# Forgetting-attention logits as three products of reduced-precision halves, with the halves made by ScalarE and GpSimd a pair of heads at a time

## The chip, the cores and the metric

The kernel runs on one NeuronCore of a Trainium2 chip. The metric is the device time of one execution in microseconds (us); smaller is better. Five engines run their own instruction queues in order and meet only at semaphores: TensorE (PE in the profile, its weight loads PEld), VectorE (DVE), ScalarE (ACT), GpSimd (POOL) and SyncE (SP, which here issues nearly all the DMAs).

## The reference

One block of a streaming encoder, batch 1, 512 tokens, 1024 channels, float32. A shared input projection feeds two branches, an mLSTM with 4 heads of 128 and a forgetting attention with 8 heads of 64; gates merge them, and an output projection and a SwiGLU feed-forward follow. The change touches only the logits of the second branch:

```python
def forgetting_attention(q, k, v, log_f):
    scale = q.shape[-1] ** -0.5
    cum = jnp.cumsum(log_f, axis=-1)
    for blk in range(s // Q_BLOCK):          # Q_BLOCK = 128
        lo = blk * Q_BLOCK; hi = lo + Q_BLOCK
        logits = (jnp.einsum("bhtd,bhsd->bhts", q[:, :, lo:hi], k[:, :, :hi]) * scale
                  + (cum[:, :, lo:hi, None] - cum[:, :, None, :hi]))
        mask = (lo + jnp.arange(Q_BLOCK))[:, None] >= jnp.arange(hi)[None, :]
        p = jax.nn.softmax(jnp.where(mask, logits, -jnp.inf), axis=-1)
        outs.append(jnp.einsum("bhts,bhsd->bhtd", p, v[:, :, :hi]))
```

## The kernel before

Weights stream from memory as granules of 128 x 1024 values into two staging buffers. ACT copies each granule to a tile of the reduced type fp32r (`w_hi`, L506), DVE subtracts that from the whole value and gets the rest, also fp32r (`w_lo`, L778), into a ring of four. PE then multiplies in three products, high by high, high by low and low by high (`three`, L1218 to L1220), each one instruction. The scores of the mLSTM heads are made in the same way from `q_hi`, `q_lo`, `k_hi`, `k_lo`.

The attention logits are not. `q_f` and `k_f` hold the scaled queries and the keys of all four pairs of heads as plain float32, a pair of heads on the 128 partitions, 64 each. `fox_logits(v)` (v = 0 to 15; pair of heads hp = v // 4, query block q) multiplies n = 128(q + 1) keys for both heads: one float32 product per head (L1442), recorded as two instructions each, on the upper and the lower 64 rows of the array; then one fp32r product per head that adds the forget-gate rows (`rows_both`, L1446), then the causal mask (L1449). The query blocks follow one another as q = 0, 1, 2, 3, 3, 2, 1, 0, so that n is 128, 256, 384, 512, 512, 384, 256, 128, twice over. Two of the eight PSUM banks are used by each step, four in turn.

On PE the order is written by hand. After the last mLSTM head (`mlstm_values(3)`, L1416) come `fox_logits(0)`, four k-steps of an output-gate projection, `fox_logits(1)`, and then `gate_piece`s: 32 pieces of three products each, of the first four gate granules, which fill the loop below. A granule's first piece takes bank 7 and waits until ACT has read the former granule out of it (`first_gate_tanh`, L644).

```python
for v in range(FOX_PAIRS):            # 16 steps
    fox_transpose(v)                  # L1463, waits for DVE's division of the probabilities
    if v + 2 < FOX_PAIRS: fox_logits(v + 2)
    if v == 0: mlstm_transpose(3)     # L1425
    for _ in range(FILL[v]): gate_piece(next(pieces))
    fox_values(v)                     # L1480, signals fox_pv
```

DVE's turn of step v: `fox_take_high` (L1059), for v = 0 `take_ymT(3)` (L944, L946, the output of the last mLSTM head), `fox_divide(v + 1)` (L1047, L1049), `fox_row_max(v + 2)` (L1036), for v = 1, 2, 6, 10 a weight half (L778). ACT's turn: for v = 2, 6, 10 the gate tanh (L644), `fox_take_low` (L640), for v = 0 `take_ymT_hi(3)` (L591), for v = 1, 2, 6, 10 a weight half (L506), `fox_softmax(v + 2)` (L630, two exponentials with their sums). POOL is nearly idle: in the mLSTM stage it squares each head's output (L472, 128 x 512) and takes a power of four values per partition (L465). ACT reaches the stage after `k_f` (L582), the floor of the stabiliser (L587) and the decays of the mLSTM heads (L609, L591, L506, L597).

## Time and profile before

| | |
|---|---|
| median of 3 runs | 780.4 us (778.96 to 780.73) |
| the profiled execution | 781.96 us |
| its span on the core | 780.2 us, 9668 instructions |
| PE busy | 768.6 us (99%) |
| DVE, ACT, POOL busy | 373.2, 257.6, 24.9 us |
| granted TensorE clock, mean | 0.996 of full |

The busy time of PE is a sum of pipelined records whose ends are modelled; what a stretch costs is read from the starts of its records or from the chain of waits. The attention stage lies between 193 and 258 us from the start of the span.

### The profile page before, as it was taken

To read this page: it belongs to the slowest core of one execution; us is meant where nothing else is said; L and a number is where in the kernel's file an instruction comes from. 1 tells how busy PE (TensorE), PEld (TensorE's weight loads), DVE (VectorE), ACT (ScalarE), POOL (GpSimd) and SP (SyncE) were. 2 spreads that over 40 slices of the span, in tenths; PEclk is the share of its full clock that TensorE was granted. 3 is DMA by queue.
4 is the path that set the end of the run, shared out by engine and by line. 5 is a ranking of instruction groups with operands and counts; after the bars stand their busy time and mean duration, and the time that the engine had idled before them with its cause. 6 is when DMAs were issued, how large, how long until landed. Compare 5 with 4: busy or idle time off the path is not lost.

```text
span 780.2 us, 9668 instructions
## 1 busy us (share of the span) xinstructions
PE 768.6 (99%) x3925; PEld 632.6 (81%) x3925; DVE 373.2 (48%) x561; ACT 257.6 (33%) x422; POOL 24.9 (3%) x50
## 2 busy tenths in 40 slices
PE   8999999999999999999999999999999999999996
PEld 7888888888576788888889888888888888888885
DVE  4678625357878525244355444433434445123224
ACT  5444222344555332233243323222323323213121
POOL 5000000012100000000000000000000000000000
PEclk9999999999999999999999999999999999999999
DMA  7324324210111134332311423332333323322302
GB/s 216 122 98 138 125 91 132 86 49 29 55 56 56 52 99 176 105 108 93 123 55 55 138 79 107 108 90 74 107 109 108 108 67 118 125 71 87 127 1 108
DMA packets 61776, 75.11 MB, mean 96 GB/s; under 512 B 3666, under 2 KB 49826, under 8 KB 61732
## 3 DMA queue, kind: packets, MB, share of 16 engines
q1 hardware_dynamic: 61728, 74.50, 29.8%
q8 instruction: 31, 0.51, 0.3%
q14 instruction: 13, 0.11, 0.0%
q10 hardware_dynamic: 4, 0.00, 0.0%
HBM read 72.40 MB, written 2.10 MB: 95 GB/s over the span
## 4 chain that ended last, share of the span: by engine, by line
PE 72%; issue 1%; DVE 0%; ACT 0%; POOLq 0%; POOL 0%; DVEq 0%; ACTq 0%
PE bank L1218 23%; PE bank L1219 22%; PE bank L1220 22%; PE bank L1480 1%; PE bank L1442 1%; PE bank L1463 1%; PE bank L1449 0%; PE bank L1231 0%; PE bank L1446 0%; ACT square_out L487 0%; DVE probs L1049 0%; ACT x L740 0%; DVE x L1190 0%; ACT ymT_hi L591 0%; DVE work L944 0%
## 5 line engine op out<-in xcount | busy, mean ns | idle before, releaser
L1218 PE MATMUL bank<-hT_hi,w_hi 128*128 128x512 f32 (+1 forms) x680 | 259.5, 382 | 1.6 <-DVE w_lo L778 1.1
L778 DVE TENSOR_TENSOR w_lo<-stage,w_hi 128x1024 fp32r<-128x1024 f32 x125 | 152.4, 1224 | 225.3 <-ACT w_hi L506 216.8
L1219 PE MATMUL bank<-hT_lo,w_hi 128*128 128x512 f32 (+1 forms) x680 | 256.7, 378 | 0.0
L1220 PE MATMUL bank<-hT_hi,w_lo 128*128 128x512 f32 (+1 forms) x680 | 256.5, 377 | 0.0
L506 ACT ACTIVATE w_hi<-stage 128x1024 fp32r<-128x1024 f32 x127 | 133.4, 1053 | 124.4 <-PE bank L1220 120.1
L1218 PEld LDWEIGHTS bank<-hT_hi,w_hi 128*128 128x128 f32 x680 | 128.2, 189 | 25.4 <-DVE w_lo L778 1.5
L1220 PEld LDWEIGHTS bank<-hT_hi,w_lo 128*128 128x128 f32 x680 | 128.1, 188 | 23.4
L1219 PEld LDWEIGHTS bank<-hT_lo,w_hi 128*128 128x128 f32 x680 | 128.3, 189 | 22.5
L1218 PE MATMUL bank<-w_hi,aT_hi 128*128 128x512 f32 x176 | 68.5, 389 | 0.0
L1220 PE MATMUL bank<-w_hi,aT_lo 128*128 128x512 f32 x176 | 68.5, 389 | 0.0
L1219 PE MATMUL bank<-w_lo,aT_hi 128*128 128x512 f32 x176 | 68.5, 389 | 0.0
L725 ACT ACTIVATE aT_hi<-work 128x512 fp32r<-128x512 f32 x22 | 13.9, 633 | 99.3 <-DVE work L1171 99.3
L1220 PEld LDWEIGHTS bank<-w_hi,aT_lo 128*128 128x128 f32 x176 | 33.1, 188 | 6.9
L1218 PEld LDWEIGHTS bank<-w_hi,aT_hi 128*128 128x128 f32 x176 | 33.1, 188 | 6.9
L1219 PEld LDWEIGHTS bank<-w_lo,aT_hi 128*128 128x128 f32 x176 | 33.1, 188 | 6.7
L721 ACT ACTIVATE work<-bank 128x512 f32<-128x512 f32 x22 | 13.2, 598 | 68.7 <-PE bank L1220 68.7
L1167 DVE SCALAR_TENSOR_TENSOR work<-work,bank 128x512 f32<-128x512 f32 x22 | 15.1, 688 | 38.5 <-PE bank L1220 38.4
L1218 PE MATMUL bank<-w_hi,mixT_hi 128*128 128x512 f32 x64 | 25.2, 393 | 0.0
L1218 PE MATMUL bank<-w_hi,hT_hi 128*128 128x512 f32 x64 | 25.2, 393 | 0.0
L445 POOL TENSOR_TENSOR rstd<-mean_sq,minus_half 128x1 f32<-128x1 f32 x12 | 6.6, 552 | 573.7 <-DVE mean_sq L749 573.3
L1220 PE MATMUL bank<-w_hi,hT_lo 128*128 128x512 f32 x64 | 24.9, 390 | 0.0
L1220 PE MATMUL bank<-w_hi,mixT_lo 128*128 128x512 f32 x64 | 24.9, 390 | 0.0
(190 smaller groups left out, 759.6 us busy)
## 6 DMA issues: line engine op xcount, KB each, us to landing
stage<-in_w_in SPq DMA_DIRECT2D x21, 1024.0 KB, 5.2
stage<-in_w_gate SPq DMA_DIRECT2D x11, 1024.0 KB, 5.3
stage<-in_w_up SPq DMA_DIRECT2D x11, 1024.0 KB, 5.4
stage<-in_w_down SPq DMA_DIRECT2D x22, 512.0 KB, 4.5
stage<-in_w_out SPq DMA_DIRECT2D x4, 1024.0 KB, 5.0
x_nat<-in_x SPq DMA_DIRECT2D x4, 512.0 KB, 5.7
stage<-in_w_br_mlstm SPq DMA_DIRECT2D x4, 512.0 KB, 3.5
stage<-in_w_br_fox SPq DMA_DIRECT2D x4, 512.0 KB, 4.5
```

Source lines behind the costliest of these rows:

```text
L445: pool.tensor_tensor(rstd[:, r:r + 1], mean_sq[:, r:r + 1], minus_half[:, 0:1], ALU.pow).then_inc(norm[i]["rstd_ready"], 1)
L506: act.activation(ring(w_hi, g), staged(g), ACT.Copy).then_inc(hi_split, 1)
L721: act.activation(work[n][:, :], psum[4 * (p % 2) + n][:, :], ACT.Tanh, scale=0.5).then_inc(ffn_tanh, 1)
L725: act.activation(aT_hi[:, f, :], work[2 + n - 2][:, :], ACT.Copy).then_inc(aT_hi_ready, 1)
L778: dve.tensor_tensor(ring(w_lo, g), staged(g), ring(w_hi, g).bitcast(F32), ALU.subtract).then_inc(lo_split, 1)
L1167: dve.scalar_tensor_tensor(out=y[:, :], in0=work[j][:, :], scalar=1.0, in1=psum[4 * (p % 2) + j][:, :], op0=ALU.add, op1=ALU.mult).then_in ...
L1218: pe.matmul(o, a_hi, b_hi, start=first, stop=False)
L1219: pe.matmul(o, a_hi, b_lo, start=False, stop=False)
L1220: return pe.matmul(o, a_lo, b_hi, start=False, stop=last)
L1442: pe.matmul(banks[h2][:, 0:n], q_f[head, hp, q * P:(q + 1) * P], k_f[head, hp, 0:n], start=True, stop=False)
L1463: ins = pe.transpose(psum[2 + low][:, c:c + HALF_ARRAY], probs[u % 4][half, j * P:(j + 1) * P], ident[half, half])
L1480: last = pe.matmul(psum[FOX_Y][h2 * DH_F:(h2 + 1) * DH_F, q * P:(q + 1) * P], v_f[:, j, c:c + DH_F], pT[:, h2, j * P:(j + 1) * P], start=( ...
```

## The change

Queries and keys of each pair of heads get tiles of their own, and each a high half of type fp32r: `qf_hi`, `kf_hi`. ACT makes them by a copy: those of pair 0 after the last `k_f` and ahead of L587; those of pair 1 ahead of `fox_softmax(0)`; those of pairs 2 and 3 at the ends of its turns v = 1 and v = 5. POOL makes the low half by subtraction, over the whole values in place: pair 0 ahead of its loop over the mLSTM heads, pairs 1, 2 and 3 behind that loop, once `fox_pv` has reached 1, 3 and 7. The high halves of pairs 1 to 3 lie where the mLSTM queries and keys were. `fox_logits` has three fp32r products per head in place of the float32 one, and waits at each new pair of heads for POOL's two subtractions.

```diff
--- before.py
+++ after.py
@@ -180,8 +180,12 @@
         R = W + 12 * K
         q_m = at("q_m", [P, H_M, SEQ], F32, R)
         k_m = at("k_m", [P, H_M, SEQ], F32, R + 8 * K)
-        q_f = at("q_f", [P, KB, SEQ], F32, R + 16 * K)
-        k_f = at("k_f", [P, KB, SEQ], F32, R + 24 * K)
+        q_f = [at(f"q_f{i}", [P, SEQ], F32, R + (16 + 2 * i) * K) for i in range(KB)]
+        k_f = [at(f"k_f{i}", [P, SEQ], F32, R + (24 + 2 * i) * K) for i in range(KB)]
+        qf_lo = [at(f"qf_lo{i}", [P, SEQ], F32R, R + (16 + 2 * i) * K) for i in range(KB)]
+        kf_lo = [at(f"kf_lo{i}", [P, SEQ], F32R, R + (24 + 2 * i) * K) for i in range(KB)]
+        qf_hi = [at(f"qf_hi{i}", [P, SEQ], F32R, R + (66 if i == 0 else 4 * i) * K) for i in range(KB)]
+        kf_hi = [at(f"kf_hi{i}", [P, SEQ], F32R, R + (68 if i == 0 else 4 * i + 2) * K) for i in range(KB)]
         o_gate = at("o_gate", [P, KB, SEQ], F32, R + 32 * K)
         ymT_hi = at("ymT_hi", [P, KB, SEQ], F32R, R + 40 * K)
         ymT_lo = at("ymT_lo", [P, KB, SEQ], F32R, R + 48 * K)
@@ -282,6 +286,7 @@
         num_m, den_step, h_m, h_squared, h_mean, h_rstd, y_m = (sem(n) for n in ("num_m", "den_step", "h_m", "h_squared", "h_mean", "h_rstd", "y_m"))
         y_mT, y_m32, ymT_hi_ready, ymT_lo_ready = (sem(n) for n in ("y_mT", "y_m32", "ymT_hi_ready", "ymT_lo_ready"))
         logits, fox_max, fox_exp, fox_norm, fox_T, fox_pv = (sem(n) for n in ("logits", "fox_max", "fox_exp", "fox_norm", "fox_T", "fox_pv"))
+        fqk_hi_ready, fqk_lo_ready = sem("fqk_hi_ready"), sem("fqk_lo_ready")
         fox_PT = [sem("fox_PT_high"), sem("fox_PT_low")]
         yfT_hi_ready, yfT_lo_ready = sem("yfT_hi_ready"), sem("yfT_lo_ready")
         gate_tanh, mix_step, mix_hi_ready, mix_lo_ready = (sem(n) for n in ("gate_tanh", "mix_step", "mix_hi_ready", "mix_lo_ready"))
@@ -456,6 +461,14 @@
 
             pool.wait_ge(norm[0]["xn_ready"], 2 * ROWS)
             pool.memset(v_m[:, :, :, DH_M:DH_M + 1], 1.0).then_inc(v_ones, 1)
+
+            def split_fox_lo(hp):
+                for n, (lo, whole, hi) in enumerate(((qf_lo, q_f, qf_hi), (kf_lo, k_f, kf_hi))):
+                    pool.wait_ge(fqk_hi_ready, 2 * hp + n + 1)
+                    pool.tensor_tensor(lo[hp][:, :], whole[hp][:, :], hi[hp][:, :].bitcast(F32),
+                                       ALU.subtract).then_inc(fqk_lo_ready, 1)
+
+            split_fox_lo(0)
             for i in range(H_M + 1):
                 if i >= 1:
                     h = i - 1
@@ -471,6 +484,9 @@
                         pool.wait_ge(h_mean, 2 * h)
                     pool.tensor_tensor(work[2][:, :], work[h % 2][:, :], work[h % 2][:, :],
                                        ALU.mult).then_inc(h_squared, 1)
+            for hp in range(1, KB):
+                pool.wait_ge(fox_pv, ROWS * (hp - 1) + (1 if hp == 1 else -1))
+                split_fox_lo(hp)
             for i in (1, 2):
                 for r in range(ROWS):
                     row_rstd(i, r)
@@ -579,10 +595,14 @@
                 if G_FQK + KB <= g < G_MO:
                     b = g - G_FQK - KB
                     act.wait_ge(used, g + 1)
-                    act.activation(k_f[:, b, :], psum[fqk_bank(KB + b)][:, :], ACT.Identity,
+                    act.activation(k_f[b][:, :], psum[fqk_bank(KB + b)][:, :], ACT.Identity,
                                    bias=vec[:, V_FQK + KB + b:V_FQK + KB + b + 1]).then_inc(fk_ready, 1)
 
 
+            act.wait_ge(fq_ready, 1)
+            act.activation(qf_hi[0][:, :], q_f[0][:, :], ACT.Copy).then_inc(fqk_hi_ready, 1)
+            act.wait_ge(fk_ready, 1)
+            act.activation(kf_hi[0][:, :], k_f[0][:, :], ACT.Copy).then_inc(fqk_hi_ready, 1)
             act.wait_ge(m_step, 1)
             act.activation(m_floor[:, :, :], m_floor[:, :, :], ACT.Exp, scale=-1.0).then_inc(floor_ready, 1)
 
@@ -615,6 +635,12 @@
                 if h < H_M - 1:
                     mo_tanh_of(h)
 
+            def split_fox_hi(hp, keys):
+                act.wait_ge(s_m, ROWS * H_M)
+                act.wait_ge(fk_ready if keys else fq_ready, hp + 1)
+                act.activation((kf_hi if keys else qf_hi)[hp][:, :], (k_f if keys else q_f)[hp][:, :],
+                               ACT.Copy).then_inc(fqk_hi_ready, 1)
+
             def take_yfT_hi(hp):
                 act.wait_ge(fox_pv, ROWS * (hp + 1))
                 act.activation(yfT_hi[:, hp, :], psum[FOX_Y][:, :], ACT.Copy).then_inc(yfT_hi_ready, 1)
@@ -653,6 +679,8 @@
 
 
             act.wait_ge(decay_exp, 10 * H_M)
+            split_fox_hi(1, False)
+            split_fox_hi(1, True)
             fox_softmax(0)
             mo_tanh_of(3)
             fox_softmax(1)
@@ -670,6 +698,9 @@
                     split_hi(G_BR + AHEAD + SPLIT_AT.index(v))
                 if v + 2 < FOX_PAIRS:
                     fox_softmax(v + 2)
+                if v % ROWS == 1 and v // ROWS + 2 < KB:
+                    split_fox_hi(v // ROWS + 2, False)
+                    split_fox_hi(v // ROWS + 2, True)
             take_yfT_hi(KB - 1)
             for n in range(len(TANH_AT), 4):
                 first_gate_tanh(n)
@@ -933,7 +964,7 @@
                     b = g - G_FQK
                     dve.wait_ge(used, g + 1)
 
-                    dve.tensor_scalar(q_f[:, b, :], psum[fqk_bank(b)][:, :], vec[:, V_FQK + b:V_FQK + b + 1],
+                    dve.tensor_scalar(q_f[b][:, :], psum[fqk_bank(b)][:, :], vec[:, V_FQK + b:V_FQK + b + 1],
                                       DH_F ** -0.5, ALU.add, ALU.mult).then_inc(fq_ready, 1)
 
             def take_ymT(h):
@@ -1428,9 +1459,9 @@
             def fox_logits(v):
 
                 hp, q = fox_pair(v)
+                if v % ROWS == 0:
+                    pe.wait_ge(fqk_lo_ready, 2 * hp + 2)
                 if v == 0:
-                    pe.wait_ge(fq_ready, KB)
-                    pe.wait_ge(fk_ready, KB)
                     pe.wait_ge(rows_low_half, 3)
                 n = (q + 1) * P
                 cols = slice(pair(q, 0) * P, pair(q, 0) * P + n)
@@ -1438,9 +1469,13 @@
                 heads = [slice(h2 * DH_F, (h2 + 1) * DH_F) for h2 in range(2)]
                 for h2 in range(2):
                     take(logit_bank(2 * v + h2), (fox_exp, 2 * v + h2 + 1))
+                rows = slice(q * P, (q + 1) * P)
                 for h2, head in enumerate(heads):
-                    pe.matmul(banks[h2][:, 0:n], q_f[head, hp, q * P:(q + 1) * P], k_f[head, hp, 0:n],
-                              start=True, stop=False)
+                    pe.matmul(banks[h2][:, 0:n], qf_hi[hp][head, rows], kf_hi[hp][head, 0:n], start=True, stop=False)
+                for h2, head in enumerate(heads):
+                    pe.matmul(banks[h2][:, 0:n], qf_hi[hp][head, rows], kf_lo[hp][head, 0:n], start=False, stop=False)
+                for h2, head in enumerate(heads):
+                    pe.matmul(banks[h2][:, 0:n], qf_lo[hp][head, rows], kf_hi[hp][head, 0:n], start=False, stop=False)
                 for h2, head in enumerate(heads):
                     lane = H_M + 2 * hp + h2
                     pe.matmul(banks[h2][:, 0:n], pick[head, lane:lane + 1].to_broadcast([DH_F, P]), rows_both[head, cols],
```

## Rows read from the trace of the kernel before

**Rows 1.** The page: busy time of each engine, chain that ended last by engine.
```profile
PE 768.6 (99%) x3925; PEld 632.6 (81%) x3925; DVE 373.2 (48%) x561; ACT 257.6 (33%) x422; POOL 24.9 (3%) x50
...
PE 72%; issue 1%; DVE 0%; ACT 0%; POOLq 0%; POOL 0%; DVEq 0%; ACTq 0%
```

**Rows 2.** PE in order of time: start, us, engine, line, what; steps of 512 and 128 keys.
```profile
212.66 1.08 PE L1442 MATMUL bank<-k_f,q_f 64*128 64x512 f32 x4
...
214.00 0.48 PE L1218 MATMUL bank<-hT_hi,w_hi 128*128 128x512 f32 x1
...
224.90 0.44 PE L1442 MATMUL bank<-k_f,q_f 64*128 64x128 f32 x4
...
225.43 0.48 PE L1218 MATMUL bank<-hT_hi,w_hi 128*128 128x512 f32 x1
```

**Rows 3.** PE in order of time: mLSTM scores, three fp32r products of each width.
```profile
173.14 0.39 PE L1220 MATMUL bank<-q_hi,k_lo 128*128 128x512 f32 x1
173.37 0.33 PE L1218 MATMUL bank<-q_hi,k_hi 128*128 128x384 f32 x1
...
173.90 0.29 PE L1218 MATMUL bank<-q_hi,k_hi 128*128 128x256 f32 x1
...
174.27 0.22 PE L1218 MATMUL bank<-q_hi,k_hi 128*128 128x128 f32 x1
...
174.55 0.63 PE L1425 MATMUL bank<-ident,work 128*128 128x128 f32 x4
```

**Rows 4.** PE in order of time, v = 0 to 3; in brackets idle before, and releaser.
```profile
204.60 0.44 PE L1480 MATMUL bank<-pT,v_f 128*64 128x128 f32 x4
206.41 0.34 PE L1463 MATMUL bank<-ident,probs 64*128 64x64 f32 x4 [1.36 <-DVE probs L1049]
206.97 0.34 PE L1463 MATMUL bank<-ident,probs 64*128 64x64 f32 x4 [0.23 <-DVE probs L1049]
207.14 1.93 PE L1442 MATMUL bank<-k_f,q_f 64*128 64x512 f32 x4
...
209.43 0.40 PE L1449 MATMUL bank<-mask_b,ident_b 128*128 128x128 bf16 x2
```

**Rows 5.** Windows: stretch, length, busy PE, PEld, DVE, ACT, POOL; then PEclk, DMA, GB/s.
```profile
209.00:210.00 1.00, 1.00 (x7) 0.58 (x4) 0.67 (x3) 0.87 (x1) 0.00 (x0) 0.50 0.00 0
...
211.00:213.00 2.00, 2.00 (x26) 1.32 (x26) 1.32 (x3) 1.62 (x6) 0.00 (x0) 1.00 0.00 0
```

**Rows 6.** DVE in order of time: what PE's wait hangs on, and the maxima of v = 3.
```profile
205.11 0.69 DVE L946 TENSOR_TENSOR ymT_lo<-work,ymT_hi 128x512 fp32r<-128x512 f32 x1 [0.69 <-ACT ymT_hi L591]
...
205.91 0.35 DVE L1049 TENSOR_SCALAR probs<-probs,row_inv 128x256 f32<-128x256 f32 x1
...
209.75 1.29 DVE L1036 TENSOR_REDUCE neg_max<-bank 128x1 f32<-128x512 f32 x2 [0.30 <-PE bank L1449]
```

**Rows 7.** POOL in order of time: a square of 128 x 512, and a power of four values.
```profile
195.46 1.04 POOL L472 TENSOR_TENSOR work<-work 128x512 f32<-128x512 f32 x1 [0.33 <-DVE work L1004]
197.93 1.01 POOL L465 TENSOR_TENSOR head_rs<-head_ms,minus_half 128x4 f32<-128x4 f32 x1 [1.43 <-DVE head_ms L966]
```

**Rows 8.** DVE in order of time, beside these two and after them.
```profile
195.69 1.35 DVE L1013 TENSOR_TENSOR work<-work,head_rs 128x512 f32<-128x512 f32 x1
...
197.95 0.29 DVE L1049 TENSOR_SCALAR probs<-probs,row_inv 128x128 f32<-128x128 f32 x1
...
199.40 0.69 DVE L1013 TENSOR_TENSOR work<-work,head_rs 128x512 f32<-128x512 f32 x1
```

**Rows 9.** ACT in order of time: a high half, and the gate tanhs of v = 2, 6.
```profile
151.28 0.62 ACT L577 ACTIVATE k_hi<-k_m 128x512 fp32r<-128x512 f32 x1
...
211.82 0.68 ACT L644 ACTIVATE work<-bank,vec_half 128x512 f32<-128x512 f32 x1
...
227.71 0.68 ACT L644 ACTIVATE work<-bank,vec_half 128x512 f32<-128x512 f32 x1
```

**Rows 10.** PE in order of time: the piece behind the tanh of v = 6.
```profile
228.64 0.48 PE L1218 MATMUL bank<-hT_hi,w_hi 128*128 128x512 f32 x1
```

## The prediction

> **What bounds the kernel now.** I read the page first: PE is busy 768.6 of 780.2 us, and the chain that ended last lies on PE for 72% of the span, DVE and ACT under 1% [rows 1]. So time comes off only where PE has less to do, and goes on wherever PE is made to wait. Then PE in order of time through the attention stage, 193 to 258 us. It falls into two parts. Up to 206 us PE is ahead: behind the values of step 0 (L1480, 204.60) it stands idle 1.36 and 0.23 us until DVE has divided the probabilities of step 1 (L1049) [rows 4]. DVE works without a pause from 193 to 202 us, and ends this part with a chain through ACT: L946 waited for ACT's high half of the last mLSTM head, and the division stands behind it in DVE's order [rows 6]. From about 211 us to the end of the stage PE has no idle record, and what it does sets the pace. Between the two lies a stretch at half clock (granted 0.50 at 209 to 210, 1.00 again from 211; 1.2 and 2.4 GHz), which follows on the two waits [rows 5].
>
> So a shorter logits step pays from v = 3 on; in v = 0 to 2 it only lengthens the wait, since DVE's chain there starts from no PE record that moves.
>
> **What the three products save on PE.** From the start of L1442 to the start of the next weight product, a step of 512 keys takes 1.34 us, one of 128 keys 0.53 [rows 2]; 0.27 per 128 keys, which is five times 128 columns at 2.4 GHz (0.053). L1446 is one fp32r product per head; the other four passes are the float32 product, with the two heads side by side on the two halves of the array (in turn they would give more than five). The new step has three fp32r passes of that kind plus L1446. A pass is dearer than its columns: the mLSTM products of 512, 384, 256, 128 columns follow each other at 0.23, 0.177, 0.123 and 0.093 us [rows 3], where the columns alone are 0.213, 0.160, 0.107, 0.053. At 512 to 256 that is 0.017 more for each instruction, and at 128 it isn't the columns that set the pace but something of about 0.1 us, which I take to be the weight load. So, of each step, one pass goes and one more instruction per head comes: 512 keys -0.213 + 0.017 = -0.196; 384: -0.143; 256: -0.09; 128: three passes at 0.093 against 0.20 of four bare passes, +0.08 (bounds: -0.04 if the two heads' loads hide, +0.11).
>
> Only v = 3 to 15 count. v = 4 to 15 have each width three times: 3 x (-0.196 - 0.143 - 0.09 + 0.08) = -1.05 us; of these v = 4 is -0.20 and v = 5 to 15 are -0.85. v = 3 took 2.29 us from L1442 to L1449, at half clock for most of it [rows 4]; a pass of 512 columns is 0.427 there, so about -0.39.
>
> **What ACT's copies cost.** A high half of 128 x 512 takes 0.62 us (L577) [rows 9]; two in a row occupy ACT about 1.08 us, because consecutive records overlap by some 0.08. Pair 0's two push the decays of head 0 and DVE's weighing from 157.5 to 158.6; their product on PE starts at 164.7, 4 us behind their end, so nothing. Pair 1's fall into ACT's 2.2 us of idle ahead of the first exponentials: nothing. Those of pair 3 stand at the end of turn v = 5, directly ahead of the gate tanh of v = 6. That tanh runs 227.71 to 228.39 [rows 9], and PE's first piece of the next granule, which needs its bank, starts at 228.64 [rows 10]: a margin of 0.25 us against an insertion of 1.08. The exponential ahead of the tanh hangs on DVE, and DVE on the transposes of v = 5, so no gain on PE moves it. The tanh ends at 229.47, PE is ready at 228.8 (two steps of 128 keys), and with 0.07 for the semaphore it waits: +0.75 us. Nothing that PE could do is behind the piece in its order but the values of v = 6.
>
> Pair 2's copies stand in the same way ahead of the tanh of v = 2 (211.82). What they cost depends on where PE is then, below.
>
> **What POOL's subtractions cost.** Eight of 128 x 512. The nearest row is POOL's square of the same size, 1.04 us (L472) [rows 7]. POOL is free, and the halves are early: pair 1 by about 208 against 213, pairs 2 and 3 some 6 us ahead. So the new wait on PE costs nothing by itself. What they do to DVE is another matter. While that square ran from 195.46 to 196.50, DVE's L1013 of the same size took 1.35 us; the same instruction alone took 0.69 at 199.40 [rows 7, 8]. It ended 0.54 us after POOL did: it stood until POOL was done. L1013 reads two tiles of SBUF. DVE's instructions with one operand in PSUM (L944, L1004) kept their time beside POOL. The division L1049 has one input, in SBUF, and takes 0.29 us for 128 columns and 0.35 for 256 [rows 6, 8], 0.06 per 128 where L1013 needs 0.69 for 512; that looks like two streams of one tile, so I put it with L1013. The row against is L1049 at 197.95, which took its usual 0.29 beside POOL's power L465, but that one touches four values per partition and may have been computing [rows 7, 8]. Bounds for a division beside a subtraction: nothing, or all that is left of the subtraction.
>
> The Trainium skill ("SBUF — State Buffer", section "SBUF: two separate sides") has this as a rule: GpSimd and VectorE share one pair of ports, locked by whoever comes first for its whole instruction, against VectorE instructions with two SBUF inputs or in a two-port mode; "VectorE: DVE Perf Modes" says that float32 `tensor_scalar` from SBUF to SBUF runs in such a mode. L1013 agrees (1.35 against 0.69); no row here shows it for L1049. By the rule the stall below is the full one, without it 0.7 us less.
>
> Where do they fall? Pair 1's two start when the values of v = 0 are done, now 205.04, then some 0.2 sooner: about 204.9. That is just ahead of L946 (two SBUF inputs) at 205.11 and of both divisions, the chain on which PE waits [rows 4, 6]. POOL 204.93 to 205.97; L946 then ends at 206.5; the second subtraction 206.5 to 207.55; L1047 beside it, the first division 207.55 to 207.9, the second to 208.5. PE's second transpose starts at 208.6, not 206.97: +1.6 (0.9 if the divisions aren't held; 0 if nothing is). Pair 2's two (about 217.5) find L778 on DVE and then a division; the transposes that need it have 1.4 us of slack: hidden. Pair 3's (about 232) find margins of 0.1 to 0.9 around the transposes of v = 8 and 9: I take +0.2, bounds 0 and 0.8.
>
> **From v = 1 to the first piece of v = 2.** Transposes at 208.6, L1442 of v = 3 at 208.8; if the half clock ends where it did (about 210.7), L1449 starts at 210.7. Two pieces now at full clock, 1.39 us where they took 2.05; values 0.59, transposes 0.42, logits of v = 4 in 1.14: PE is ready for the first piece of v = 2 at 214.4. ACT: the maxima of v = 3 on DVE come 1.6 later less their 0.30 of idle [rows 6], so the tanh shifts from 211.82 by 1.3, and by 1.08 for pair 2's copies, and ends at 214.9. PE starts the piece at 214.95; it was 214.00 [rows 2]: +0.95, in which the savings of v = 3 and 4 are contained.
>
> **Sum** against the profiled execution (781.96 us; span 780.2): +0.95 (up to v = 2) - 0.85 (v = 5 to 15) + 0.75 (tanh of v = 6) + 0.2 (pair 3) = +1.05 us. That execution was 1.56 above the median of the runs, so on the median it is 780.4 + 1.05 = 781.5 us. No change that can be told: a difference under about 0.2%, 1.6 us, is what this measurement can't separate from none.
>
> **The rivals.**
> *POOL holds DVE nowhere (or only L946).* Then PE's wait stays, v = 3 and 4 give 0.59, the tanh of v = 2 still makes its margin (it ends 213.4 against 213.4), the rest stays: -0.59 - 0.85 + 0.75 = -0.7, 779.7. For: L1049 at 197.95. Against: L1013. Chance 0.18.
> *All savings land*: as before, and ACT's copies cost nothing either: -1.44, or -1.8 with the steps of 128 keys at their lower bound: 778.6. Against: the order of ACT's queue and the margin of 0.25. Chance 0.07.
> *The slow side: the half clock lasts.* It came after 1.59 us of idle within 2 us [rows 4, 5]; now the idle is some 3.2 us long and reaches to 208.3, and a second stretch of the length of the first (3.3 us) could follow on it. Then the two pieces take 2.56 rather than 1.39 and the values and transposes 0.2 more, half a microsecond of which ACT's wait would have taken anyway: +1.0 more, 782.5; pair 3's stall at its upper bound brings it to 783.1. It decides if the longer idle keeps the clock from coming back at 210.7. Chance 0.25.
> *The heads run in turn.* Three more passes per step, 0.16 us per 128 keys, 30 such units in v = 4 to 15: +4.8, 786.3. Against: L1446 is an fp32r product per head, and five passes in all leave it no turn [rows 2]. Chance 0.04.
> *It doesn't do what it says*: PE waits for the low halves at v = 4, 8 or 12, because ACT's copy or the subtraction comes late. Each such wait would be about 1 to 2 us; 783.5. By the times above they are 5 us early. Chance 0.02.
>
> **How the numbers follow.** The forecast holds 0.44, its own range 780.2 to 782.3 (stall 0.9 instead of 1.6; pair 3's bound). The chances 0.44, 0.18, 0.07, 0.25, 0.04, 0.02. Faster by over 1.6 us: 0.09 (all savings, and 0.02 of the first rival). Slower by over 1.6: 0.36 (the clock, heads in turn, late halves, and 0.05 of the forecast's upper end). Within: 0.55. The range leaves out the heads in turn and half of the case in which all savings land: 778.7 to 784.2.
>
> **What the profile afterwards would show.** L1442's successors: three lines, x2 each per step, with a step of 512 keys about 1.14 from its first product to the weight product, one of 128 keys about 0.6. PE's wait ahead of the transposes of v = 1 near 3 us, with L946 or L1049 longer than 0.69 and 0.35 beside the two POOL records at 205 to 207.5. PE idle ahead of the first piece of v = 6, released by ACT's L644. PEclk at half for one stretch near 208 to 211, or for two. I am wrong if DVE's records beside POOL keep their time, or if PE shows no wait on the tanh.

## The result and the profile after

The changed kernel takes 783.54 us (median, 783.17 to 784.31) where the kernel before took 778.97 (778.96 to 780.73) beside it: 4.6 us between the medians. The ratio with its 95% interval is 1.0051 (1.0037 to 1.0065), a little under that of the medians. Forecast were 781.5 us and "no change that can be told". It is slower by 0.5%, which is a change that can be told; the time is inside the range, near its upper end, and on the side that had 0.36. The profiled execution took 783.4 us with a span of 781.7.

The page of the kernel after, busy time by engine and the chain that ended last, to be read against [rows 1]:

```profile
PE 768.6 (98%) x3957; PEld 635.1 (81%) x3957; DVE 376.4 (48%) x561; ACT 261.2 (33%) x430; POOL 36.4 (5%) x58
...
PE 70%; issue 2%; DVE 2%; ACT 1%; POOLq 0%; POOL 0%; DVEq 0%; ACTq 0%
```

PE has the same busy time, but its share of the chain fell by 2 points, and DVE and ACT have 3 that they did not have. PE is made to wait for them. The view of waits says where (after; line that waited, releaser, total us, times, longest):

```profile
PE bank L1498 <- DVE probs L1080: 3.1, 3, 2.2
...
PE bank L1249 <- ACT work L670: 0.5, 1, 0.5
```

L1498 are the transposes (L1463 before), L1080 the division (L1049), L670 the gate tanh (L644), L1249 the weight product (L1218). The first row was 1.6 us in two waits, the second did not exist. After, PE in order of time, v = 0 to 3, which answers to [rows 4]:

```profile
203.24 0.44 PE L1515 MATMUL bank<-pT,v_f 128*64 128x128 f32 x4
205.84 0.47 PE L1498 MATMUL bank<-ident,probs 64*128 64x64 f32 x4 [2.16 <-DVE probs L1080]
207.02 0.48 PE L1498 MATMUL bank<-ident,probs 64*128 64x64 f32 x4 [0.71 <-DVE probs L1080]
207.25 0.78 PE L1474 MATMUL bank<-kf_hi,qf_hi 64*128 64x512 f32 x2
...
209.24 0.40 PE L1484 MATMUL bank<-mask_b,ident_b 128*128 128x128 bf16 x2
```

The two waits were 1.36 and 0.23 us and are 2.16 and 0.71. What DVE and POOL did meanwhile (after; both in order of time, against [rows 6, 7]):

```profile
203.73 0.69 DVE L977 TENSOR_TENSOR ymT_lo<-work,ymT_hi 128x512 fp32r<-128x512 f32 x1 [0.70 <-ACT ymT_hi L611]
...
204.53 1.16 DVE L1080 TENSOR_SCALAR probs<-probs,row_inv 128x256 f32<-128x256 f32 x1
...
205.99 0.97 DVE L1080 TENSOR_SCALAR probs<-probs,row_inv 128x256 f32<-128x256 f32 x1
```

```profile
203.76 1.77 POOL L468 TENSOR_TENSOR qf_lo<-q_f,qf_hi 128x512 fp32r<-128x512 f32 x1 [6.21 <-PE bank L1515]
205.50 1.31 POOL L468 TENSOR_TENSOR kf_lo<-k_f,kf_hi 128x512 fp32r<-128x512 f32 x1
```

DVE's subtraction L977 came 0.03 us ahead of POOL's and kept its 0.69; POOL's took 1.77 instead of 1.3. Then it was DVE's turn to be held: its two divisions took 1.16 and 0.97 us where one takes 0.35, and ended some 0.15 us after POOL's instructions did (205.53 and 206.81).

The windows of after (stretch, length, busy PE, PEld, DVE, ACT, POOL; PEclk, DMA, GB/s), against [rows 5]:

```profile
206.00:207.00 1.00, 0.31 (x4) 0.12 (x3) 1.00 (x2) 0.00 (x0) 0.81 (x1) 0.50 0.00 0
211.00:212.00 1.00, 1.00 (x4) 0.49 (x2) 0.99 (x1) 1.00 (x4) 0.00 (x0) 0.50 0.00 0
212.00:213.00 1.00, 1.00 (x11) 0.59 (x12) 0.00 (x0) 1.00 (x3) 0.00 (x0) 0.79 0.00 0
```

The granted clock is half from 205.6 to 212.4, some 6.8 us, where the profile of before had 3.4 (3.3 in the prediction, read from coarser windows). Its first 1.4 us, to 207.02, are the end of the first wait (0.25 us), the transposes of one head and the second wait (0.71 us), so PE has next to nothing to run there.

**The ruler for all that follows.** The attention stage is taken from PE's first product that spreads the mLSTM maxima to its first product on `ymT_hi`; times inside it count from that start. It is 154.99 to 258.26 before, 153.64 to 259.68 after: 103.27 and 106.04 us, +2.77. The profiled executions differ by 1.44 only, since that of before had lost 1.35 us more ahead of the stage, 1.1 of it in one wait for `w_lo` that the trace of after does not have. Four times in each trace, worked out from the first logits product of a step and from the end of the stage; idle is that ahead of the transposes of v = 1, "half" the length of the half clock in the attention stage of that profiled execution. One execution each of e0, e3 and e9 lies far outside the others (4377, 851 and 1094 us) and is left out of the ratios:

| kernel | idle | half | v = 3 | v = 5 | end | v = 5 to end | median us | ratio to before, 95% |
|---|---|---|---|---|---|---|---|---|
| before | 1.59 | 3.4 | 52.15 | 61.92 | 103.27 | 41.35 | | |
| after | 2.87 | 6.8 | 53.61 | 63.76 | 106.04 | 42.28 | 783.54 | 1.0051 (1.0037 to 1.0065) |
| e1 | 1.60 | none | 52.13 | 61.19 | 103.43 | 42.24 | 781.12 | 1.0016 (1.0007 to 1.0024) |
| e2 | 3.0 | 6.8 | 53.61 | 64.13 | 105.67 | 41.54 | 782.92 | 1.0036 (1.0023 to 1.0049) |
| e3 | 1.6 | 3.4 | 52.11 | 61.43 | 102.19 | 40.76 | 778.52 | 0.9982 (0.9971 to 0.9993) |
| e4 | 1.59 | none | 52.12 | 60.15 | 100.90 | 40.75 | 779.82 | 0.9989 (0.9979 to 1.0000) |
| e5 | 0.23 | none | 52.12 | 60.15 | 100.90 | 40.75 | 779.00 | 0.9981 (0.9971 to 0.9991) |
| e6 | 0.2 | none | 52.17 | 60.20 | 101.54 | 41.34 | 779.60 | 0.9994 (0.9983 to 1.0005) |
| e7 | 3.00 | 6.8 | 53.68 | 64.54 | 105.92 | 41.38 | 783.18 | 1.0033 (1.0023 to 1.0043) |
| e8 | 0.23 | none | 52.11 | 59.72 | 100.48 | 40.76 | 778.45 | 0.9979 (0.9968 to 0.9990) |
| e9 | 0.23 | none | 52.15 | 59.91 | 101.29 | 41.38 | 778.92 | 0.9982 (0.9972 to 0.9992) |
| e10 | 2.57 | none | 53.13 | 61.27 | 102.65 | 41.38 | 781.16 (one run) | |
| e11 | 1.80 | none | 52.37 | 60.52 | 101.88 | 41.36 | 781.31 (one run) | |

### The profile page after: what moved, and what is told of

It reads as the page before. It is cut to its first block, busy times and chain, and to the rows that moved or that the text cites. A ratio compares the mean times of both kernels' runs of the same rounds, so it can differ in the third digit from the quotient of the medians.

```text
span 781.7 us, 9756 instructions
## 1 busy us (share of the span) xinstructions
PE 768.6 (98%) x3957; PEld 635.1 (81%) x3957; DVE 376.4 (48%) x561; ACT 261.2 (33%) x430; POOL 36.4 (5%) x58
## 4 chain that ended last, share of the span: by engine, by line
PE 70%; issue 2%; DVE 2%; ACT 1%; POOLq 0%; POOL 0%; DVEq 0%; ACTq 0%
PE bank L1249 22%; PE bank L1251 22%; PE bank L1250 22%; PE bank L1515 1%; DVE probs L1080 1%; PE bank L1498 1%; DVE neg_max L1067 0%; PE bank L1262 0%; DVE row_inv L1078 0%; PE bank L1474 0%; PE bank L1484 0%; ACT probs L656 0%; PE bank L1481 0%; PE bank L1478 0%; PE bank L1476 0%
## 5 line engine op out<-in xcount | busy, mean ns | idle before, releaser
L1249 PE MATMUL bank<-hT_hi,w_hi 128*128 128x512 f32 (+1 forms) x680 | 259.5, 382 | 1.3 <-POOL w_lo L457 0.7
L1249 PEld LDWEIGHTS bank<-hT_hi,w_hi 128*128 128x128 f32 x680 | 128.3, 189 | 25.0 <-POOL w_lo L457 0.9
L1249 PE MATMUL bank<-w_hi,aT_hi 128*128 128x512 f32 x176 | 68.5, 389 | 0.0
L1249 PEld LDWEIGHTS bank<-w_hi,aT_hi 128*128 128x128 f32 x176 | 33.0, 188 | 6.9
L1249 PE MATMUL bank<-w_hi,mixT_hi 128*128 128x512 f32 x64 | 25.1, 393 | 0.0
L1249 PE MATMUL bank<-w_hi,hT_hi 128*128 128x512 f32 x64 | 25.1, 393 | 0.0
```

Of the source, the lines that this page charges most:

```text
L1249: pe.matmul(o, a_hi, b_hi, start=first, stop=False)
```

## The experiments

**e0: how far the kernel before scatters.** No edit.

> The kernel before, once more, for its profile. Its runs lie in two groups, near 779.0 and 780.4 to 780.7 us; the profiled one (781.96) shows a wait of 1.1 us on a weight half at 36.7 us and a half-clock stretch of 3.3 us at 207 to 211, worth 1.6 us. Theory A: the runs near 779.0 are those without the stretch and without that wait, so a profile of about 779 has a span near 777.2, PEclk 1.00 throughout the attention stage, and T of the first piece of v = 2 some 1.6 us earlier in the stage. Rival: the stretch is in every run, and only the wait at 36.7 us comes and goes (then a span near 778.9).

Ratio 0.9999 (0.9990 to 1.0008). Its profile is of the execution of 4377 us and tells nothing of this stage. What it was meant to show came from the granted clock that every run carries. Over the three sets of runs with the experiments the kernel before ran 82 times: 45 runs have a mean clock of 0.998 or more and a median of 779.5 us, 37 have 0.996 or 0.997 and a median of 781.15; over all 82 it is 780.0. The two groups are 1.64 us apart, which is about half of the 3.4 us of half clock in the profile. So the same waits are sometimes followed by the stretch and sometimes not, and the kernel before has two usual times. The mean is a coarse sign of it: every profile in the table also ends at half clock, for 0.9 to 3.3 us of its span, so that a single 0.997 can be either. Of the other nine runs of e0 seven have 0.998 or more and two 0.996. The profile of before was one of the dearer kind; the five runs beside the result happened to be mostly of the cheaper one.

**e1: pair 1's halves during the mLSTM part.** Against after:

```diff
+                if i == 2:
+                    split_fox_lo(1)                 # POOL, in the loop over the mLSTM heads
-            for hp in range(1, KB):
+            for hp in range(2, KB):
...
+                if h == H_M - 1:
+                    split_fox_hi(1, False)          # ACT, ahead of the last decays
+                    split_fox_hi(1, True)
```

> The changed kernel, with pair 1's high halves copied ahead of head 3's decays and its low halves subtracted on POOL behind the power of head 1 (about 186 to 189 us), where DVE has no instruction with two SBUF inputs. Theory A (POOL's two subtractions at 203.8 to 206.8 hold DVE's two divisions, and the longer idle of PE prolongs the half clock): the wait ahead of the transposes of v = 1 goes from 2.16 + 0.71 back to about 1.5 + 0.2 us, L1080 at 256 columns takes 0.35 and not 1.16 and 0.97, the half-clock stretch is 3.4 us or none; 783.5 - 1.4 - 1.7 = 780.4, between 779.0 and 782.1. Rival (the divisions are late for another reason, or the three products are what costs): 783 or more.

781.12 us, 2.4 less than after. The divisions are back at 0.35 us, PE's waits at 1.37 and 0.23, and v = 3 starts at 52.13 instead of 53.61: POOL's two subtractions there were worth 1.48 us, 1.27 of it idle and 0.2 in the two transposes, which ran at half clock in after (0.47 and 0.48 us for 0.34). Six of its eleven runs have a mean clock of 0.998 or more and five 0.996, against 0.994 to 0.996 in after. But the gain meets the next thing in line. PE in order of time in e1:

```profile
211.77 0.47 PE L1252 MATMUL bank<-hT_hi,w_hi 128*128 128x512 f32 x1 [1.03 <-ACT work L675]
```

and ACT ahead of it, with pair 2's copies in front of the tanh:

```profile
209.90 0.63 ACT L625 ACTIVATE qf_hi<-q_f 128x512 fp32r<-128x512 f32 x1
210.42 0.62 ACT L625 ACTIVATE kf_hi<-k_f 128x512 fp32r<-128x512 f32 x1
210.94 0.68 ACT L675 ACTIVATE work<-bank,vec_half 128x512 f32<-128x512 f32 x1
```

In after, the half clock made PE late enough to hide this wait of v = 2. So the two losses overlap: from v = 3 to v = 5 e1 takes 9.06 us with the wait and at full clock, after 10.15 with the half clock and no wait, and e4 8.03 with neither.

**e2: the copies behind the tanh.** Against after:

```diff
-                if v + 2 < FOX_PAIRS:
-                    fox_softmax(v + 2)
-                if v % ROWS == 1 and v // ROWS + 2 < KB:
+                if v % ROWS == 2 and v // ROWS + 2 < KB:
                     split_fox_hi(v // ROWS + 2, False)
                     split_fox_hi(v // ROWS + 2, True)
+                if v + 2 < FOX_PAIRS:
+                    fox_softmax(v + 2)
```

> The changed kernel, with pair 2's and pair 3's high halves copied behind the gate tanh of v = 2 and v = 6 instead of ahead of it. Theory A (ACT's copies hold up the tanh, and PE's first piece of v = 6 waits for it): no idle of PE ahead of that piece (it was 0.54, and 0.83 later in the stage), tanh 1.08 us earlier; 783.5 - 0.8 = 782.7. The copies now stand ahead of the exponentials of v + 2, which had 1 us of idle: nothing back. Rival: the wait only moves to the transposes of v = 8, since DVE is late there: 783.3 to 783.7.

The wait for the tanh of v = 6 is gone, and with it 0.74 us between v = 5 and the end (42.28 to 41.54). Up to v = 5 e2 is 0.37 us later than after, so half of it does not reach the end. The holds and the length of the half clock are as in after; but it begins 52.85 us into the stage against 51.95, 0.9 us later, so that less of it falls in the waits and more on work.

**e3: pairs 2 and 3 without halves.** As e1, and the copies and subtractions of pairs 2 and 3 are left out; their logits are made from pair 1's halves, so the work of PE is that of the change and the logits of two pairs are not the reference's.

```diff
-                    pe.matmul(banks[h2][:, 0:n], qf_hi[hp][head, rows], kf_hi[hp][head, 0:n], start=True, stop=False)
+                    pe.matmul(banks[h2][:, 0:n], qf_hi[min(hp, 1)][head, rows], kf_hi[min(hp, 1)][head, 0:n], start=True, stop=False)
```

> As e1, but pairs 2 and 3 use the halves of pair 1: their four copies on ACT and four subtractions on POOL are left out (so the logits of these pairs are not the right ones); PE's instructions are the same. Theory A: against e1 the wait on the tanh (0.8) and the one on the divisions of v = 9 (0.4) go: 1.2 us less than e1, 779.2 if e1 is 780.4. What is then left against the kernel before is PE's own saving, -0.45 us in v = 4 to 15 by the starts of the records. Rival (the copies and subtractions hide, the products cost): equal to e1.

This is the price list of the three products: from v = 5 to the end 40.76 us against 41.35, so they save 0.59 us there. It is 0.2% faster than before, 0.9982 (0.9971 to 0.9993). Beside it, after loses 42.28 - 40.76 = 1.52 us in the same part. Step by step 0.75 of it lies between the logits of v = 8 and 9 (the tanh of v = 6), 0.57 between v = 10 and 11, and 0.19 between v = 12 and 13. The 0.57 are pair 3's subtractions: e2, which moves the copies and leaves the subtractions, still has them (3.76 us for this step against 3.18 in e3), and e4 below, which moves both, has 3.18. After, POOL and DVE in order of time:

```profile
232.24 1.29 POOL L468 TENSOR_TENSOR qf_lo<-q_f,qf_hi 128x512 fp32r<-128x512 f32 x1 [11.88 <-PE bank L1515]
233.48 1.30 POOL L468 TENSOR_TENSOR kf_lo<-k_f,kf_hi 128x512 fp32r<-128x512 f32 x1
```

```profile
232.85 0.77 DVE L1080 TENSOR_SCALAR probs<-probs,row_inv 128x128 f32<-128x128 f32 x1
...
233.91 0.95 DVE L1080 TENSOR_SCALAR probs<-probs,row_inv 128x128 f32<-128x128 f32 x1
```

0.29 each without POOL [rows 8]. That everything later on DVE and ACT shifts until PE stands for it at v = 11 (238.63, 0.23 us idle) is read from the order of the rows, not tested by itself.

**e4: the halves where nobody divides.** Pairs 1 and 2 are subtracted on POOL in the mLSTM part, pair 3's two behind the transposes of v = 4 and v = 8, one each; all copies stand on ACT around the decays of the last mLSTM head, ahead of the attention steps. Against after (POOL's part of the edit):

```diff
+                    split_fox_lo(1)
+                    split_fox_lo(2)
...
+            for n, v in enumerate((4, 8)):
+                pool.wait_ge(fox_T, 2 * (v + 1))
+                split_fox_lo(3, (n,))
```

> The changed kernel with all its halves, none at the places that cost: high halves of pairs 1 to 3 on ACT around head 3's decays (184 to 190 us), low halves of pairs 1 and 2 on POOL between 184 and 190, those of pair 3 one at a time as the transposes of v = 4 and v = 8 are done. PE's instructions are those of the changed kernel. Theory A (port, clock and ACT's order are all that the change costs): like e3, in which the copies and subtractions of pairs 2 and 3 were left out, so 778.5 to 779, 1 us below the kernel before; no PE wait on a tanh, waits ahead of the transposes of v = 1 of 1.4 and 0.2 us. Rival: the copies and subtractions cost wherever they stand (decays or the square of head 2 late): 780 to 781.

All three losses are gone: 1.59 us of idle, no wait for a tanh, 40.75 from v = 5 to the end. The eight halves are all made, so they cost nothing there. The median is 0.9989 of before (0.9979 to 1.0000), because 7 of its 12 runs have the clock of 0.996 or 0.997 (779.7 to 780.7) and 5 that of 0.999 (778.15 to 779.24). The 778.5 to 779 us that were expected came only in these.

**e5: work into the wait.** On e4, the two weight pieces of v = 1 moved up, from behind its transposes to ahead of them:

```diff
-FILL = (3, 2) + (2,) * 6 + (2, 2, 1, 2, 2, 1, 1, 1)
+FILL = (5, 0) + (2,) * 6 + (2, 2, 1, 2, 2, 1, 1, 1)
```

> As e4, and the two gate pieces of v = 1 moved up behind those of v = 0 (FILL 5, 0 instead of 3, 2), so that PE has 1.4 us more to do while DVE finishes the divisions of v = 1. Theory A: PE's wait of 1.6 us shrinks to 0.2 there and 0.5 ahead of the next transposes, and with it goes the half-clock stretch that the profiled kernel before had: e4 less 1.0 where there was no stretch, up to 2.6 where there was; 777. Rival (DVE's chain of v = 1 and 2 sets the pace whatever PE does first): equal to e4.

The stage is as long as in e4 to the hundredth, 100.90: the idle of 1.36 went from one place to two others. The waits of e5:

```profile
PE bank L1257 <- ACT work L683: 0.8, 1, 0.8
...
PE bank L1523 <- ACT pT L679: 0.6, 1, 0.6
```

What did change is the clock: all 12 runs have 0.998 or more, and the median went from 779.8 to 779.0. The gain of filling is that no stretch follows, not that the wait is used. The 777 us that were expected did not come.

**e6: the same filling on the kernel before.** The diff of e5 alone, on before.

> The kernel before with the same two pieces moved up (FILL 5, 0). Theory A: as between e4 and e5, 1.0 to 1.6 us less than before, 778.5, and no half-clock stretch. Rival: equal to before. The difference of e5 to e6 is then what the three products bring without the stall and without the clock: about 0.6 to 1 us.

779.60 (778.5 was expected), all 12 runs at 0.998 or 0.999. Against e5 the whole change is worth 0.64 us of stage at full clock (101.54 and 100.90) and 0.6 us of median, which the scatter of the 12 and 12 runs leaves standing.

**e7: POOL's two subtractions alone on the kernel before.** Nothing else of the change; their results are read by nobody:

```diff
+            pool.wait_ge(fox_pv, 1)
+            for n, t in enumerate((q_f, k_f)):
+                pool.tensor_tensor(spare[n][:, :], t[:, 1, :], t[:, 2, :], ALU.subtract).then_inc(spare_done, 1)
```

> The kernel before, with two subtractions of 128 x 512 added on POOL when the values of v = 0 are done, where pair 1's stand in the changed kernel; they write to a spare place, nobody but ACT much later waits for them. Theory A (the shared port, then the clock): L1049 at 256 columns takes about 1.1 and 1.0 us instead of 0.35, PE waits 2.2 + 0.7 instead of 1.4 + 0.2 us, the half clock lasts about 6.6 us in the profile instead of 3.3; time +1.4 to +3.1 against before. Rival (POOL harmless, the stall comes from ACT's or PE's new work): no difference.

783.18 us, nearly all of the loss. POOL and DVE in e7:

```profile
203.68 1.78 POOL L478 TENSOR_TENSOR spare<-q_f 128x512 fp32r<-128x512 f32 x1 [6.20 <-PE bank L1486]
205.42 1.31 POOL L478 TENSOR_TENSOR spare<-k_f 128x512 fp32r<-128x512 f32 x1
```

```profile
204.44 1.16 DVE L1055 TENSOR_SCALAR probs<-probs,row_inv 128x256 f32<-128x256 f32 x1
...
205.91 0.97 DVE L1055 TENSOR_SCALAR probs<-probs,row_inv 128x256 f32<-128x256 f32 x1
```

The same two durations as in after, waits of 2.16 and 0.84 on PE, half clock from 206.2 to 213.1, and a stage 2.65 us longer than before with not one product changed. From v = 5 on it is the kernel before (41.38).

**e8: the next wait in line.** On e5, the gate tanh of the first piece of v = 2 one ACT turn earlier:

```diff
-TANH_AT = (2, 6, 10)
+TANH_AT = (1, 6, 10)
```

> The kernel e5_spread_fill (halves of pairs 1 to 3 made in other places, one more weight piece ahead of the transposes of v = 1) with one more change: ACT takes the gate tanh of the first piece of v = 2 one turn earlier. In e5 PE waited 0.8 us for that tanh ahead of its next weight piece, and 0.6 us for ACT's copy of the probabilities. Theory: the wait on the tanh is a matter of ACT's order alone; it goes, PE's share of it (0.5 to 0.8 us) comes off the stage (100.9 to about 100.3 us), and the median goes from 779.0 to about 778.3. Rival: DVE's chain to the probabilities of v = 1 ends last anyway, since ACT's tanh now stands ahead of an exponential; the 0.8 us come back as a wait on DVE or on the copy of the probabilities: stage 100.9 us, median 779.0. Either way the clock is at full speed through the stage, and both lie below the kernel before by 0.1 to 0.2%.

The wait for the tanh is gone, the one for ACT's copy of the probabilities grew from 0.55 to 1.14 us, and 0.42 of the 0.8 us come off the stage (100.48). The median is 778.45, 0.21% below before (0.10 to 0.32%): the lowest here, though e3, e5 and e9 lie within this interval.

**e9: both shifts on the kernel before.**

> The kernel before with the same two shifts and nothing of the change: one more weight piece ahead of the transposes of v = 1 (that is e6_before_fill, 779.6 us), and the gate tanh of the first piece of v = 2 one ACT turn earlier. Theory that the three products are worth 0.5 to 0.7 us at full clock, whatever stands around them: this kernel is slower than e8_spread_fill_tanh by that much, its stage near 101.0 us against 100.3. Rival: the gain of e8 comes from the shifts and the products are worth nothing; then the two agree to 0.2 us. If the tanh's shift gives nothing, this one is 779.6 as e6 was.

778.92 us, 0.9982 (0.9972 to 0.9992). Most of e8's gain over before is therefore had without the change. Between e8 and e9 lie 0.81 us of stage, 0.62 of it from v = 5 on. Their medians are 0.47 us apart, which eight and ten runs do not separate from none: what the products are worth beside e8 rests on the two traces.

**e10: a POOL instruction that only writes.** On e7:

```diff
-                pool.tensor_tensor(spare[n][:, :], t[:, 1, :], t[:, 2, :], ALU.subtract).then_inc(spare_done, 1)
+                pool.memset(spare[n][:, :], 0.0).then_inc(spare_done, 1)
```

> The kernel e7_before_pool_pair1 (the kernel before, and on POOL two subtractions of 128 x 512 after the values of v = 0, whose results nobody reads), with each subtraction replaced by a POOL memset of 128 x 1408 of about the same length, which reads nothing. In e7 DVE's two divisions of 256 columns took 1.16 and 0.97 us instead of 0.35, and PE waited 2.16 and 0.84 us ahead of its transposes. Theory A, any POOL instruction holds the port: the first division takes about 1 us again and PE waits some 3 us. Theory B, only a POOL instruction that reads two operands holds it: both divisions at 0.35 us, PE waits 1.36 and 0.23 us as in the kernel before, and one stretch at half clock of about 3.3 us or none.

POOL and DVE in e10 (the first memset ran from 204.94 to 206.21, the second to 207.57):

```profile
204.94 2.63 POOL L478 MEMSET spare<- 128x1408 f32 x2 [6.17 <-PE bank L1486]
```

```profile
204.93 0.69 DVE L952 TENSOR_TENSOR ymT_lo<-work,ymT_hi 128x512 fp32r<-128x512 f32 x1 [0.70 <-ACT ymT_hi L596]
...
205.73 0.62 DVE L1055 TENSOR_SCALAR probs<-probs,row_inv 128x256 f32<-128x256 f32 x1
...
206.66 1.05 DVE L1055 TENSOR_SCALAR probs<-probs,row_inv 128x256 f32<-128x256 f32 x1
```

Theory A: a memset, which reads nothing, holds the division until it ends, both times. But the first one ran beside DVE's subtraction of two tiles, and neither took longer (1.27 us, where the second memset took 1.42, and the usual 0.69), where a POOL subtraction had been held by it for 0.5 us in after. The Trainium skill ("SBUF — State Buffer", section "Who interferes with whom") says just this: a VectorE instruction with two SBUF inputs contends only with GpSimd instructions that read SBUF, one in a two-port mode with all of them. The 2.57 us of idle (some 3 were expected) were followed by no half clock in this one run.

**e11: POOL's work in quarters.** On e7, each subtraction cut into four of 128 columns:

```diff
-                pool.tensor_tensor(spare[n][:, :], t[:, 1, :], t[:, 2, :], ALU.subtract).then_inc(spare_done, 1)
+                for c in range(0, SEQ, P):
+                    pool.tensor_tensor(spare[n][:, c:c + P], t[:, 1, c:c + P], t[:, 2, c:c + P],
+                                       ALU.subtract).then_inc(spare_done, 1)
```

> The kernel e7_before_pool_pair1 with each subtraction of 128 x 512 cut into four of 128 x 128, eight instructions in a row. Theory, a division waits for the end of the one POOL instruction that holds the port and then goes ahead of the next: a quarter is about 0.35 to 0.45 us, so each of the two divisions, and the subtraction of L946 ahead of them, is held for no more than that; the divisions take 0.4 to 0.8 us each, and PE waits at most 0.8 us more than in the kernel before (1.6 us there, 3.0 in e7). Rival: POOL's next instruction takes the port again before DVE gets it; then the divisions are held as long as the whole row of eight, one of them takes over 1.5 us, and PE waits 3 us or more.

PE in e11:

```profile
207.15 0.34 PE L1471 MATMUL bank<-ident,probs 64*128 64x64 f32 x4 [1.36 <-DVE probs L1057]
207.93 0.34 PE L1471 MATMUL bank<-ident,probs 64*128 64x64 f32 x4 [0.44 <-DVE probs L1057]
```

The first division kept its 0.35 us, the second took 0.57, so DVE does get in between two POOL instructions (both divisions ended 0.15 us after a quarter did), and the two subtractions cost PE 0.21 us instead of 1.41. POOL pays: eight quarters took 4.14 us together against 3.05 of the two whole ones in e7, most of them 0.45 to 0.50 each. This is one run, at a mean clock of 0.998, and its 781.31 us say nothing of the cost: its stage begins at 155.73, 2.1 us later than that of after, and is as long as that of before at full clock but for 0.2.

## Why the prediction was wrong where it was

The terms of the sum, as forecast and as the traces have them (from the table, against before):

| term | forecast | measured |
|---|---|---|
| up to v = 5 (forecast at the first piece of v = 2, measured at the logits of v = 5) | +0.95 | +1.84 |
| savings of the products from v = 5 on | -0.85 | -0.59 |
| copies ahead of the tanh of v = 6 | +0.75 | +0.75 |
| pair 3's subtractions | +0.2 | +0.57 and +0.19 |
| sum | +1.05 | +2.76 (the stage: +2.77) |

**The step that failed: "if the half clock ends where it did".** The mechanism of POOL and the divisions was right, and its size too: the second transposes were forecast 1.6 us later, v = 3 starts 1.46 later, and e7 gives all of this without the products. The order was another one (DVE's L977 came first and held POOL, not the reverse) and a subtraction takes 1.3 us, not the 1.04 of the square; the two nearly cancel. But the prediction let the longer idle be followed by the old stretch of half clock. It was followed by twice its length: it began at 205.6, ahead of both transposes, and ended at 212.4, so that 5.2 us of work behind the start of v = 3 ran at half clock where 1.9 were forecast. Of the rival in which the half clock lasts, at 0.25, this was the mechanism, and its forecast for the first piece of v = 2, +1.95, is nearly what came: 214.50 in after, whose stage begins 1.35 us sooner, against 214.00 in [rows 2], which makes +1.85. With pair 3 at its upper bound this rival stood at 783.1. From v = 3 to v = 5, 8.14 us pass at full clock (e10, 8.15 in e11), 9.77 in the profile of before and 10.15 in after.

**The base hid a second state of the same thing.** The prediction scaled from the profiled execution, which had the stretch, to the median of three runs, one of which, by its time, did not have it. At full clock the stage of before is 101.64 us: 103.27 less 1.63, and e10 and e11 less their extra idle of 0.98 and 0.21 give 101.67 both. Against this the change costs 4.4 us, and that is what the medians beside the result show (783.54 - 778.97 = 4.6); against the median of the 82 runs, 780.0, it is 3.5. After has the low clock in all five of its runs (0.994 to 0.996), before in 37 of 82. So the change not only lengthens a stretch that is there; it brings, in all five runs, a stretch that came in less than half of those of before. The views of before could not say this; its three times, 780.73, 780.40 and 778.96, could have raised the question.

**Why the number was still inside the range.** That was luck in part. The difference was forecast at +1.05 us and came out at +4.6 against the runs of before beside it; the time missed by 2.0 us only because the base, 780.4, was 1.4 above the 778.97 of these. The forecast's own branch ended at 782.3. What held 783.54 was the width that the other branches gave the range.

**The savings were over-counted by 0.26 us.** After, PE in order of time, a step of 512 and one of 128 keys, to be read as [rows 2]:

```profile
213.28 0.49 PE L1474 MATMUL bank<-kf_hi,qf_hi 64*128 64x512 f32 x2
...
214.50 0.47 PE L1249 MATMUL bank<-hT_hi,w_hi 128*128 128x512 f32 x1
...
225.22 0.30 PE L1474 MATMUL bank<-kf_hi,qf_hi 64*128 64x128 f32 x2
225.37 0.27 PE L1476 MATMUL bank<-kf_lo,qf_hi 64*128 64x128 f32 x2
...
225.89 0.47 PE L1249 MATMUL bank<-hT_hi,w_hi 128*128 128x512 f32 x1
```

From the first product to the weight product it is 1.22 us (1.20 elsewhere) against 1.34, and 0.67 against 0.53: -0.14 and +0.14 where -0.196 and +0.08 were forecast. Steps of 384 and 256 keys give -0.10 and -0.05 for -0.143 and -0.09. From the first product to the mask the old step of 512 keys takes 1.24 us where its columns alone are 1.07, the new one 1.11 to 1.13 for 0.85: the new form carries 0.08 to 0.1 us more beside its columns, and the forecast had 0.017 for this. In the new form the later passes of two heads follow each other at 0.23 to 0.24 us, close to their columns (0.213), but the first takes 0.32. The short step paces at 0.11 to 0.15 us a pass. Counted so, v = 5 to 15 would save 0.31; the stage shows 0.59 (and the same 0.6 in e4 against e6), so some 0.3 us of it lie outside these intervals. From the logits of one step to those of the next, e4 against e10, the steps save 0.17 us at 512 keys, 0.10 to 0.13 at 384, 0.06 to 0.10 at 256 and lose 0.08 to 0.13 at 128: the missing part is some 0.03 in each step, between the weight product and the next logits. Why it is there no run shows.

**The two smaller terms.** The tanh of v = 6 came as worked out (0.75 for 0.75), a margin and an insertion read from two rows; the step from the tanh's end to PE's start was 0.15 us (229.78 to 229.93) where the forecast had 0.07, and the two copies took 1.04 where it had 1.08. Pair 3's holds came at the upper bound of 0.8: DVE's margin was taken as that of one division, but both were held, by 0.48 and 0.66 us, and the tail reached the third tanh. That the products save something at all is shown by e3, e4, e5 and e8; that the change as written loses it is due to where POOL's instructions stand, by e7.

## What to carry to other kernels

Work handed to GpSimd cost nothing here only where VectorE ran nothing, in that time, that shares its port (e4 against e7); check each GpSimd instruction against the VectorE instruction that the critical engine waits for, and move it, or cut it into short ones. An idle spell on TensorE has two prices, its own length and the half clock that may follow, and the second comes in some runs and not in others: compare the granted clock of the runs before you take one profile as the base of a sum. And an offset of a microsecond here or there may be hidden or released by the next wait in line: with the holds gone the tanh appeared (e1), with that gone the copy of the probabilities (e8).

## What the hardware did that was not expected

- A GpSimd subtraction of two tiles of 128 x 512 with an fp32r result takes 1.29 to 1.31 us alone, a square of one tile 1.04 [rows 7]; which of the two differences costs the 0.25 was not tried. A quarter of it takes mostly 0.45 to 0.50, not 0.33 (e11, one run).
- A VectorE division by a per-partition scalar, float32 with its one tile in SBUF, is held by each GpSimd instruction tried, whole and quarter subtractions and one that only writes, and ends about 0.15 us after it at 256 columns, 0.09 at 128 (pair 3). In the trace of before one was not, beside a power of four values [rows 7, 8].
- Idle of 1.59 us on PE is followed by half clock in about half of the runs (by the mean clock of each run, which is coarse: 37 of 82 before, 5 of 11 in e1, 3 of 11 in e3, 7 of 12 in e4), idle of 2.87 or more in nearly all (all five of after at 0.994 to 0.996, of e2 at 0.994 to 0.997; in e7 10 of 12 by the same measure), and with 0.23 there and waits of up to 1.14 us further on, work between them, in one of 42 at most (e5, e6, e8, e9, that one at 0.997 and still one of the fastest times). The sum of the waits is as large in e5 as in e4 (1.60 and 1.58 us): what differs is that they stand apart. In e10 2.57 us were followed by none.
